# Group rows stored in chunk order by the copy out of PSUM, so that the gather matmuls load dense columns

## The reference, cut to what matters

```python
def hier_moe(h, w_grp, b_grp, w_exp, b_exp, w1, w3, w2):
    # 32 experts in 4 groups of 8: top-1 group, then top-2 experts in it, for each of the 256 tokens
    ...
    def expert_block(args):
        tok_b, w_b, e = args
        xb = t[tok_b]                                  # gather the rows of expert e
        hid = jax.nn.silu(xb @ w1[e]) * (xb @ w3[e])   # 1024 -> 512, twice
        return (hid @ w2[e]) * w_b[:, None]            # 512 -> 1024
    ...
    out = jnp.zeros((T, D)).at[buf_tok].add(ys)        # back to the tokens
```

## Time and profile before

| what | value |
|---|---|
| time, median of 3 runs | 2337.78 us (2336.65 to 2340.24) |
| the profiled execution's own time | 2339.84 us |
| its span, first to last instruction | 2338.0 us |
| TensorE busy | 2318.0 us (99% of the span) |
| weight loads (PEld) busy | 1434.5 us (61%), overlapping TensorE |
| VectorE / ScalarE / GpSimd busy | 1052.4 / 463.3 / 74.4 us |
| mean granted TensorE clock | 0.996 |
| the two expert stages | about 1100 to 1568 us and 1859 to 2327 us |

### The profile page before, as it was taken

One profiled execution on the slowest core, in us unless ns is written; L12 is line 12 of the kernel. 1 busy time (PEld: TensorE's weight loads), 2 busy tenths in 40 slices (PEclk: granted clock), 3 DMA queues, 4 the chain that ended last, 5 costly groups with the idle time before them and its releaser, 6 DMA issues.

```text
span 2338.0 us, 26668 instructions
## 1 busy us (share of the span) xinstructions
PE 2318.0 (99%) x11270; PEld 1434.5 (61%) x11270; DVE 1052.4 (45%) x2070; ACT 463.3 (20%) x1035; POOL 74.4 (3%) x131
## 2 busy tenths in 40 slices
PE   9999999999999999999999999999999999999998
PEld 6579448875695469995444444437999544444443
DVE  4478656667687467682111111225767211111122
ACT  3311003366110011221111111110122111111111
POOL 2000000010100000000000000000000000000000
PEclk9999999999999999999999999999999999999999
DMA  7378625354797333339999999964343999999993
GB/s 288 139 318 364 278 77 201 145 202 179 271 377 321 140 140 132 153 122 401 395 427 429 426 428 428 425 237 181 123 153 133 390 400 428 427 428 427 427 426 118
DMA packets 59316, 672.50 MB, mean 288 GB/s; under 512 B 7520, under 2 KB 7808, under 8 KB 18864
## 3 DMA queue, kind: packets, MB, share of 16 engines
q1 hardware_dynamic: 51888, 649.45, 67.7%
q0 software_dynamic: 7296, 21.21, 2.7%
HBM read 667.37 MB, written 3.26 MB: 287 GB/s over the span
## 4 chain that ended last, share of the span: by engine, by line
PE 96%; DVE 2%; DMA 1%; issue 0%; ACT 0%; POOL 0%; SPq 0%; DVEq 0%; POOLq 0%; ACTq 0%
PE ps L101 94%; DVE arena L117 1%; PE ps L350 1%; DMA arena<-ssm_rows 1%; PE ps L3006 1%; DVE arena L114 0%; PE ps L639 0%; DMA ring<-in_attn_w_in 0%; PE ps L2139 0%; DVE X L117 0%; ACT arena L106 0%; PE ps L1328 0%; PE ps L2981 0%; PE ps L2965 0%; POOL small L117 0%
## 5 line engine op out<-in xcount | busy, mean ns | idle before, releaser
L101 PE MATMUL ps<-arena 128*64 128x512 f32 (+5 forms) x4580 | 1136.2, 462 | 5.8 <-DVE arena L117 4.0
L101 PEld LDWEIGHTS ps<-arena 128*128 128x128 f32 (+2 forms) x4580 | 593.8, 184 | 422.0 <-issue 389.2
L101 PE MATMUL ps<-ring,arena 128*64 128x512 f32 (+2 forms) x1592 | 502.7, 584 | 0.0
L101 PE MATMUL ps<-XTGB,ring 128*128 128x256 f32 (+1 forms) x2032 | 382.6, 344 | 0.0
L101 PEld LDWEIGHTS ps<-XTGB,ring 128*128 128x128 f32 x2032 | 333.5, 191 | 43.8 <-issue 9.9
L101 PEld LDWEIGHTS ps<-ring,arena 128*64 128x64 f32 (+1 forms) x1592 | 184.1, 152 | 240.5 <-issue 236.2
L122 DVE COPY arena<-ps 128x512 f32<-128x512 f32 (+5 forms) x133 | 63.3, 496 | 460.6 <-PE ps L101 292.4
L121 ACT COPY arena<-ps 128x512 f32<-128x512 f32 (+3 forms) x187 | 85.0, 473 | 696.3 <-PE ps L101 290.8
L117 DVE TENSOR_TENSOR arena<-ps,arena 128x256 f32<-128x256 f32 (+5 forms) x290 | 127.2, 476 | 117.5 <-PE ps L101 87.7
L101 PE MATMUL ps<-XTGB,arena 128*128 128x128 f32 (+2 forms) x736 | 178.4, 396 | 0.0
L101 PE MATMUL ps<-ring,XTGB 128*128 128x512 f32 (+3 forms) x484 | 168.0, 501 | 0.7 <-DMA ring<-in_attn_w_in 0.5
(11 more groups left out here) (158 smaller groups left out, 1054.6 us busy)
## 6 DMA issues: line engine op xcount, KB each, us to landing
arena<-in_exp_w SPq DMA_DIRECT2D x96, 2048.0 KB, 18.3
ring<-in_exp_w SPq DMA_DIRECT2D x64, 2048.0 KB, 18.1
ring<-in_mlp_w SPq DMA_DIRECT2D x25, 2048.0 KB, 11.7
ring<-in_ada_w SPq DMA_DIRECT2D x20, 2048.0 KB, 9.7
XTGB<-in_exp_w SPq DMA_DIRECT2D x16, 2048.0 KB, 16.5
ring<-in_ssm_w_in SPq DMA_DIRECT2D x12, 2048.0 KB, 7.4
ring<-in_w_in SPq DMA_DIRECT2D x12, 2048.0 KB, 7.8
ring<-in_gate_w SPq DMA_DIRECT2D x12, 2048.0 KB, 8.1
```

Of the source, the lines that this page charges most:

```text
L101: return self.e.matmul(o, lhsT=lhsT, rhs=rhs, start=start, stop=stop, skip_group_check=True)
```

## The change

ScalarE's copy writes `xr` in chunk order: from the PSUM bank, where a half's 512 features stand in natural order, it reads every eighth element (64 of them for each of the eight chunks) and writes eight dense runs of 64. `xr` then holds chunk `c` in columns 128c to 128c+127, and the gather's stationary operand is a dense slice. Nothing else is edited: the same instructions in the same order with the same semaphores.

```diff
-        xr_q = xr.rearrange("p (q c) -> p q c", c=8)
+        xr_q = xr.rearrange("p (c q) -> p c q", c=8)
...
                 for c in range(c0, c0 + (4 if i else 2)):
-                    ins = pe.mm(ps[:, (c - c0) * P:(c - c0 + 1) * P], xr_q[:, :, c], psel, True, True)
+                    ins = pe.mm(ps[:, (c - c0) * P:(c - c0 + 1) * P], xr[:, c * P:(c + 1) * P], psel, True, True)
...
-                    act.then_inc(act.cp(xr[:, n * 512:(n + 1) * 512], ps_of("xr", l, g, n)), ("xr ready", l, g, n),
+                    act.then_inc(act.cp(xr_q[:, :, n * 64:(n + 1) * 64],
+                                        ps_of("xr", l, g, n).rearrange("p (q c) -> p c q", c=8)), ("xr ready", l, g, n),
                                  ("read", "xr", l, g, n))
```

## The result

The changed kernel takes 2284.28 us (median of 6 runs, 2282.28 to 2286.12) against 2338.04 us (6 runs, 2334.95 to 2340.24) of the kernel before beside it: ratio 0.977, 95% interval 0.9757 to 0.9783, or 53.8 us less. Forecast were 2282.0 us and 55.8 us less. The profiled execution took 2282.28 us with a span of 2280.4, so its span is 57.6 us shorter than the one of before. Six runs against six say 53.8. Most of the difference is TensorE's clock: in the profiled execution of before, the granted clock fell to half (1.2 of 2.4 GHz) ahead of both expert stages and at the start of the second, and in the one of after it did not at these places.

The account below looks back on a forecast made before the run. TensorE (99% busy) and, side by side in the expert stages, the weight stream through full DMA engines bound the kernel. Savings of 27.9 us a layer, 55.8 together, take the median from 2337.8 to 2282.0 us, range 2280 to 2285.

Parts of the forecast that it names:

- The gather's saving: TensorE's gather in each pair: sixteen records fall from 3.68 to 1.78 us, 1.9 us saved, 16 gathers a layer.
- The rival that the distance is not the cause: Gather loads stay at 334 ns and only the copies get dearer, +1.4 us: 2339 us, chance 4%.
- Why the distance costs: Gather loads: 334 ns put down to column distance, since loads four elements apart take 212 and dense ones 192.
- The copy: ScalarE's rearranging copy out of PSUM: +0.7 us, only the second copy of group 0 being on the path.
- the front: From the first matmul of gather(0) to w1 of pair 0: 2.1 us saved less 0.7 for the copy, 1.4 us.
- The slower rival: The strided copy out of PSUM takes so long that the kernel loses, from 7.6 us a copy: 2359 us, chance 1%.
- The stream's shift: Expert weight transfers from matrix 15 on start 3.3 us earlier (1.4 + 1.9), at an unchanged pace.
- The cap: Weights limit TensorE's lead in the last pairs: a 2.0 us wait at pair 14, leaving 27.9 us a layer.
- The rival without a cap: The stream starts earlier than thought or the copy costs nothing more: 61.2 us saved, 2277 us, chance 8%.
- the rival: The 2 us wait halves TensorE's clock for about 5 us, 2.5 us a layer: 2287.0; 8% chance includes cap without shift.
- The sum: Whole kernel: 27.9 + 27.9 = 55.8 us saved over both layers, median from 2337.8 to 2282.0 us.

Follow-up runs that it names:

- light weights: Only two of four chunks of each exp_w2 matrix of pairs 0 to 14 transferred, used twice: changed kernel 2278.21 us, kernel before 2339.14 us.
- the layouts above: Changed kernel with xr columns 16 bytes apart: 2337.37 us; 8 bytes: 2285.1 us; 12 bytes (last two chunks 8): 2300.81 us.

## Why the prediction was right, point by point

**The gather's saving: right.** Forecast 1.9 us each, measured 1.89 from pair to pair, and 28.4 / 15 = 1.9 with light weights. The rival that the distance is not the cause is refuted by the layouts above; so is the rule of the page "TensorE: Matmul & The Clock Gate" of the Trainium skill, section LDWEIGHTS, that a load's time follows from its columns alone: the same 128 columns took 192 to 334 ns here.

**Why the distance costs: the step behind it was wrong, though the term stood.** "A load from columns four elements apart takes 212 ns, between the dense one and the one eight apart" compared two different things. The earlier trace rows are transposes, whose dense load takes 140 ns, so 212 was already a slow load, not a middle one, and a transpose pays less for the distance than a gather. The gather's own load at that distance takes 330. That the term came out right is luck as far as this step goes: dense and eight apart had each been read from rows. Had the change been a layout of four elements, the same reasoning would have forecast 50 us and won nothing. A dense transpose to compare with was in reach of the argument and was not looked for.

**The copy: mis-sized, +0.7 us forecast, 0 measured.** I took the 1278 ns of the earlier trace rows, an ACTIVATE from SBUF to SBUF, for a read from PSUM; the lower end of the bounds, 586 ns, was right. What the row's price consists of these runs do not settle, but of the copies tried only those paid that write SBUF 16 bytes or more apart. It leaves the front at 2.0 us instead of 1.4, a difference of 0.6 in each layer. The slower rival, which needed 7.6 us for a copy, fell far off.

**The stream's shift: 3.3 us forecast, 4.1 measured at matrix 15 and 3.3 at matrix 85.** The transfer of matrix 15, beside the earlier trace rows:

```profile
L248 SPq DMA_DIRECT2D ring<-in_exp_w x1: 327/327/327, 1127.8 to 1127.8; - x1
...
DMA to landing us min/median/max: 9.8/9.8/9.8
```

It is issued 5.2 us earlier than before and lands 5.4 us earlier; 1.25 us of that were already there at the first copy ahead of pair 0 (1098.95 before, 1097.69 after) and are the clock fall of the execution before. The rest is 4.1: the 3.3, and the copy that cost nothing. "And with it everything after it" held only in part: single transfers took some tenths longer, and at matrix 85 (1486.5 before, 1482.0 after) 3.3 us are left of it. Why is open.

**The cap: right in kind and place, too small in layer 1.** Forecast was a wait of 2.0 us in each layer, at w1 of pair 14 in layer 0 and of pair 15 in layer 1, "pairs 12 and 13 wait a few tenths". Measured were 2.8 and 4.2 us, spread over w3 of pairs 12 and 13 and w1 of pairs 14 and, in layer 1, 15 (up to 1.5 us each). The weights' slack shrank by what TensorE won, and pairs 12 and 13 ran out first. Layer 1 is where the forecast was off. At matrix 91 it allowed a lead of 24.6 + 1.9 = 26.5 us within the stage. The matrix landed 33.3 us earlier (2275.2 to 2241.9) and the stage began 32.2 us earlier (1864.3 to 1832.1), a shift of 1.1 instead of 1.9, so 25.7 were allowed; 25.4 were measured. And 1.2 of these are not saved by the change but by the clock, which fell at 1863.20 in the execution before; the 1.00 of the earlier trace rows is the mean of the whole stage and hides it. So the term that was too small is the wait in layer 1: 2.0 us forecast, 4.2 measured. The rival without a cap is the run with light weights: 2278.2 us measured, 2277 forecast.

**The clock: no fall in this profile, but the rival stands.** In the changed kernel it is 1.00 in every window of the stages, with waits of up to 1.5 us in the last pairs. In the kernel that reads `X` in pairs, which is as fast, TensorE waited 2.1 us for w1 of pair 15 in layer 1, and then was granted half the clock:

```profile
2243.29 3.60 PE L101 MATMUL ps<-ring,arena 128*64 128x512 f32 x8 [2.08 <-DMA ring<-in_exp_w]
```

```profile
2243.20:2246.60 3.40, 3.31 (x8) 1.12 (x10) 0.00 (x0) 0.00 (x0) 0.00 (x0) 0.51 1.02 424
```

An estimate from these rows: eight records in 3.4 us, where sixteen fit at 0.21 us each, cost 1.7 us, less than the 2.5 a layer that the rival assumed. The forecast also took the 0.72 us of idle time before gather(0) as harmless, from layer 0; in layer 1 of the kernel before the same idle time was followed 3 us later by a clock of 0.50. Whether the one caused the other isn't shown.

**The sum.** The spans differ by 3.3 (up to w1 of pair 0 in layer 0), 25.7 (stage), 3.2 (to w1 of pair 0 in layer 1), and 25.4 (stage): 57.6 us. As an estimate, the clock falls of the execution before make up 1.25 of the first, 1.1 of the third (from the end of the first stage to ScalarE's second copy of the next it took 291.4 us before and 290.3 after) and 1.2 of the fourth. Without them the change gave 2.0 + 25.7 in layer 0 and 2.1 + 24.2 in layer 1, 54.0 us, where 1.4 + 26.5 was forecast for each. In layer 0 the two errors cancel (27.7 against 27.9), which is luck. In layer 1 they do not (26.3 against 27.9), and that is most of what the forecast of the median, 2282.0 against 2284.3, was too low by.

## What to carry to other kernels

Read a slow fp32 matmul by the number of 16-byte lines that its operands touch: in these runs two elements in every line gave nearly the full rate (196 against 192 ns a load, 0.46 against 0.43 us a record of 512 moving columns), and one element a line about half of it. For transposes look again, since they paid far less. Put the rearrangement where it is free, which here is the read side of the copy out of PSUM, not its write side and not the matmul. Before counting a saving fifteen times, follow the stream that feeds the engine: a slack of 21 us was used up at pair 12, and 6 us of 61 were lost to it. And before taking one profile apart to tenths of a microsecond, list where its clock fell.

## What the runs showed of the hardware that was not expected

- The gather's fp32 loads of 128 columns: 192, 196, 262, 330 and 334 ns for columns 4, 8, 12, 16 and 32 bytes apart. The cost begins where a 16-byte line holds fewer than two columns.
- A transpose's load of 128 columns: 140 ns dense, 211 with columns 16 bytes apart, and only 0.01 to 0.03 us more from one to the next.
- A neighbour paid as well. The load of `turn_w` (L2981), whose own operand was not touched, took a median of 269 ns behind a slow gather and 143 behind a dense one. I take it for queueing behind the load ahead of it; no run tests that apart.
- ScalarE reads PSUM every 32 bytes in 0.585 us for 512 elements, as fast as densely; VectorE's multiply, which reads one factor from SBUF and one from PSUM 16 bytes apart, goes from 0.69 to 1.06 us. Which of its two reads costs that was not tried.
